# Chunked delta-rule recurrence and block attention of a three-block network: another factoring of the recurrence, attention by pairs of heads

## Reference, cut to what matters

```python
def rwkv7_mixer(ya, ...):            # 6 heads of 64 channels
    ...
    def step(state, inp):
        r_t, w_t, k_t, v_t, kk_t, a_t = inp
        sa = jnp.einsum('bhij,bhj->bhi', state, -kk_t)
        state = (state * w_t[:, :, None, :]
                 + sa[..., :, None] * (kk_t * a_t)[:, :, None, :]
                 + v_t[..., :, None] * k_t[:, :, None, :])
        return state, jnp.einsum('bhij,bhj->bhi', state, r_t)
    ...
def moba_mixer(q, k, v):             # 6 heads of 64 channels
    ...                              # with 2 blocks of 256 keys and top 3, every past block is taken:
                                     # plain causal attention over 512 tokens
```

## Time and profile before

| | us |
|---|---|
| median of 3 runs | 3279.8 (3279.63 to 3281.37) |
| profiled execution, first to last instruction (span) | 3270.9 |
| median less span | 8.9 |
| the stage that changes (first score to last attention output, 1701.8 to 1806.1) | 104.3 |
| PE busy in that stage | 103.22 |
| DVE / ACT busy in that stage | 38.88 / 30.84 |

### The profile page before, as it was taken

How to read it: one execution, slowest core, us unless ns; L and a number is a source line. 1 busy time by engine, 2 the same in 40 slices (tenths; PEclk the granted TensorE clock), 3 DMA queues, 4 the chain that set the end, 5 groups by cost and what they waited for, 6 DMA issues and landing times.

```text
span 3270.9 us, 35828 instructions
## 1 busy us (share of the span) xinstructions
PE 3179.8 (97%) x14634; PEld 1976.4 (60%) x14634; DVE 1372.5 (42%) x2564; ACT 598.2 (18%) x1240; POOL 1.4 (0%) x6
## 2 busy tenths in 40 slices
PE   8999999999999999999999999999999999999998
PEld 5855554334333433458786588888546444688887
DVE  4256530111111111165743364466353894364655
ACT  2143220110010001121442320102332002120001
POOL 0000000000000000000000000000000000000000
PEclk9999999999999999999997999999999999999999
DMA  6122369999999999931000222222111222222221
GB/s 268 60 78 93 114 250 411 428 428 429 429 428 429 429 428 429 428 138 37 26 1 1 93 87 78 86 95 103 55 52 52 77 77 77 77 78 103 78 78 52
DMA packets 43100, 585.39 MB, mean 179 GB/s; under 512 B 4768, under 2 KB 6816, under 8 KB 7648
## 3 DMA queue, kind: packets, MB, share of 16 engines
q1 hardware_dynamic: 42752, 582.45, 43.8%
q0 software_dynamic: 224, 1.18, 0.1%
HBM read 581.51 MB, written 2.10 MB: 178 GB/s over the span
## 4 chain that ended last, share of the span: by engine, by line
PE 87%; DMA 9%; DVE 3%; ACT 1%; issue 1%; SPq 0%; DVEq 0%; ACTq 0%
PE PS L482 20%; PE PS L294 11%; PE PS L1670 11%; PE PS L686 10%; DMA ring<-in_weights 5%; PE PS L1648 4%; DMA A<-in_weights 4%; PE PS L1246 3%; PE PS L374 2%; PE PS L1593 2%; PE PS L348 2%; PE PS L1634 1%; PE PS L1575 1%; PE PS L2198 1%; PE PS L1038 1%; PE PS L1203 1%
## 5 line engine op out<-in xcount | busy, mean ns | idle before, releaser
L482 PE MATMUL PS<-A 128*128 128x256 f32 x1336 | 298.4, 380 | 0.0
L1670 PE MATMUL PS<-ring,A 128*64 128x512 f32 x1248 | 284.8, 599 | 1.5 <-DMA ring<-in_weights 0.6
L482 PEld LDWEIGHTS PS<-A 128*128 128x128 f32 x1336 | 254.1, 190 | 35.1 <-issue 0.8
L294 PE MATMUL PS<-H,ring 128*128 128x512 f32 x544 | 234.4, 593 | 0.7 <-issue 0.7
L1752 DVE TENSOR_TENSOR A<-A,PS 64x512 f32<-64x512 f32 x64 | 44.1, 690 | 434.6 <-ACT A L1699 434.6
L482 PE MATMUL PS<-H,ring 128*128 128x256 f32 x784 | 185.3, 380 | 0.8 <-ACT A L1785 0.8
L1670 PEld LDWEIGHTS PS<-ring,A 128*64 128x64 f32 x1248 | 82.7, 136 | 168.0 <-issue 160.8
L294 PEld LDWEIGHTS PS<-H,ring 128*128 128x128 f32 x544 | 103.5, 190 | 130.0 <-issue 130.0
L1670 PE MATMUL PS<-A 128*64 128x512 f32 x784 | 178.4, 598 | 2.0 <-DMA A<-in_weights 0.8
L686 PE MATMUL PS<-A 128*128 128x256 f32 x800 | 178.7, 379 | 0.0
L1648 PE MATMUL PS<-A 128*64 128x512 f32 x768 | 174.3, 598 | 3.4 <-DMA A<-in_weights 3.1
(11 more groups left out here) (534 smaller groups left out, 4126.9 us busy)
## 6 DMA issues: line engine op xcount, KB each, us to landing
ring<-in_weights SPq DMA_DIRECT2D x176, 2048.0 KB, 14.2
A<-in_weights SPq DMA_DIRECT2D x96, 2048.0 KB, 24.3
X<-in_x SPq DMA_DIRECT2D x1, 2048.0 KB, 12.9
H<-in_weights SPq DMA_DIRECT2D x1, 2048.0 KB, 13.6
A<-in_weights SPq DMA_DIRECT2D x2, 768.0 KB, 23.8
vec<-in_vec SPq DMA_DIRECT2D x1, 1047.0 KB, 11.1
A<-in_ctx SPq DMA_DIRECT2D x1, 1024.0 KB, 19.1
out_y<-X SPq DMA_DIRECT2D x2, 512.0 KB, 2.9
```

The source lines that it names most:

```text
L294: mm = nc.tensor.matmul(bank[:, 0:out_width], weight_tile(name, n), moving(k), start=k == 0, stop=k == k_tiles - 1)
L482: mm = nc.tensor.matmul(pair_bank(name, p, n), w[:, k, :], x[:, k, :], start=k == 0 and not more, stop=k == 3, skip_group_check=more)
L1670: mm = nc.tensor.matmul(PS[CAP * up:CAP * (up + 1), c % 2, :], XS[:, k, CAP * b:CAP * (b + 1)], expert_tile(slot, 8 * (k % 4) + 4 * up), s ...
```

## The change

Recurrence. The walk over the chunks goes. In its place:

- `keys_turned`: 12 transposes bring the decayed keys of `KR` to tokens on partitions; ACT copies them (3 copies of 128x512) to `KTOK`.
- `values_seen`: 24 products (128x128 weights, 64 columns moving), as L2619 before; 4 ACT copies of 128x384 to `WVTOK`.
- `solved`: 24 products of the inverse with 128 columns moving, 64 of `WVTOK` and 64 of `KTOK` side by side; 6 ACT copies of 128x512 into slot 2 of SC2.
- `gains`: 12 products that, with an identity added by DVE, give a 64x64 matrix by head for chunks 1 and 2; the state then goes from chunk to chunk by `carried` (6 products of 64x64 weights with 64 columns, twice), on top of `added` (36 products, as L2633 and L2634 before, three groups of 12). DVE scales each of three states out of PSUM (`state_kept`).
- `queries_solved`: 18 products of 128 rows by 64 columns, 128 moving, which DVE adds to the queries in `KR` (`query_kept`, 3 times).
- `outputs`: by pair of heads, 16 products of 128 rows by 64 columns and then 6 of 64x64 with the states, 128 moving each; 3 ACT copies of 128x512.

Attention. The unit order is now by pair of heads: units 2k and 2k+1 are the same query tile of the two heads of a tile. Step k (12 of them) is: the two scores of step k+1, at k = 4 and 8 the outputs of the last pair (eight matmuls that alternate between the heads), the transposes of unit 2k, a piece of the recurrence, the transposes of unit 2k+1, a second piece. A pair's output leaves in one ACT copy of 128x512. DVE takes normalise and maximum in turn.

```diff
@@ -2288,53 +2288,92 @@
...
+        def moba_place(u):
+            return 2 * (u // 8) + u % 2, u % 8 // 2
+
...
+            if u >= 2:
+                pe.wait_ge(S["att_exp"], u - 1)
...
+        def moba_output(pe, p):
+            pe.wait_ge(S["att_turned"], 8 * p + 8)
+            if p:
+                pe.wait_ge(S["att_heads"], p)
             for kt in range(TT):
...
+                for h in (2 * p, 2 * p + 1):
+                    mm = nc.tensor.matmul(PS[half64(h), 7, kt * P:], MVTOK[:, kt, 64 * h:64 * h + 64],
+                                          MPT[h % 2][:, kt, kt * P:], start=kt == 0, stop=True, skip_group_check=kt > 0)
             mm.then_inc(S["att_out"], 1)
...
+        def moba_step(pe, k, first, second):
+            if k + 1 < UNITS2 // 2:
+                moba_score(pe, 2 * k + 2)
+                moba_score(pe, 2 * k + 3)
+            if k and k % 4 == 0:
+                moba_output(pe, k // 4 - 1)
+            moba_turn(pe, 2 * k)
+            first()
+            moba_turn(pe, 2 * k + 1)
+            second()
...
+        def moba_step_act(act, k):
+            for u in (2 * k, 2 * k + 1):
+                moba_turned_act(act, u)
                 if u + 2 < UNITS2:
...
+                    moba_exp_act(act, u + 2)
+            if k and k % 4 == 0:
+                moba_leave_act(act, k // 4 - 1)
+
...
+        def moba_step_dve(dve, k):
+            for u in (2 * k, 2 * k + 1):
+                moba_normalise_dve(dve, u)
                 if u + 2 < UNITS2:
...
+                    moba_max_dve(dve, u + 2)
@@ -2483,8 +2522,10 @@
...
-        WU = (a(46)[:, 0:384], a(47)[:, 0:384])
-        STATE = a(48)[:, 0:192].rearrange("p (a i) -> p a i", a=3)
+        KTOK, WVTOK = tok384(A[:, 46:49, :]), tok384(A[:, KT2:KT2 + 3, :])
+        GAIN = a(46)[:, 0:384].rearrange("p (c a i) -> p c a i", c=2, a=3)
+        EYE64 = a(47)[:, 0:64]
@@ -2604,47 +2645,107 @@
...
+            def keys_turned(p):
+                for c in range(4):
+                    mm = nc.tensor.transpose(PS[:, p, c * P:(c + 1) * P], KR[p][:, c, 0, :], ident)
+                mm.then_inc(S["formed"], 1)
+
+            def values_seen(c):
...
+                for h in range(6):
+                    i = slice(64 * h, 64 * h + 64)
+                    mm = nc.tensor.matmul(PS[:, c % 3, i], SC2[h][:, c, 2, :], TOK2[0][:, c, i], start=True, stop=True)
+                mm.then_inc(S["formed"], 1)
...
+            def solved(h):
...
+                    tile, at = divmod(384 * c + 64 * h, T)
+                    both = A[:, KT2 + tile:47 + tile:43, at:at + 64]
+                    mm = nc.tensor.matmul(PS[:, (h + 1) % 3, c * P:(c + 1) * P], SC2[h][:, c, 0, :], both,
+                                          start=True, stop=True)
+                mm.then_inc(S["formed"], 1)
...
+            def gains():
...
+                for c in (1, 2):
+                    for h in range(6):
+                        mm = nc.tensor.matmul(PS[half64(h), 1, 192 * c - 192 + 64 * (h // 2):192 * c - 128 + 64 * (h // 2)],
+                                              SC2[h][:, c, 2, 64:], TOK2[1][:, c, 64 * h:64 * h + 64], start=True, stop=True)
+                mm.then_inc(S["chain"], 1)
...
+            def added(bank, at, c, opens):
+                for src in range(2):
+                    for h in range(6):
+                        i = slice(64 * h, 64 * h + 64)
+                        l, r = (TOK2[1][:, c, i], SC2[h][:, c, 2, 0:64]) if src == 0 else (TOK2[2][:, c, i], TOK2[0][:, c, i])
+                        mm = nc.tensor.matmul(PS[half64(h), bank, at + 64 * (h // 2):at + 64 * (h // 2) + 64], l, r,
+                                              start=opens and src == 0 and h < 2, stop=True,
+                                              skip_group_check=not (opens and src == 0 and h < 2))
+                mm.then_inc(S["chain"], 1)
...
+            def carried(c, bank, at):
+                pe.wait_ge(S["state"], c + 1)
+                for h in range(6):
+                    rows, p = half64(h), h // 2
+                    mm = nc.tensor.matmul(PS[rows, bank, at + 64 * p:at + 64 * p + 64], GAIN[rows, c - 1, p, :],
+                                          STATES[c - 1][rows, p, :], start=False, stop=True, skip_group_check=True)
+                mm.then_inc(S["chain"], 1)
...
+            def queries_solved(p):
...
+                for c in (1, 2, 3):
+                    for h in (2 * p, 2 * p + 1):
+                        mm = nc.tensor.matmul(PS[half64(h), 2, (c - 1) * P:c * P], SC2[h][:, c, 2, 64:], SC2[h][:, c, 1, :],
+                                              start=True, stop=True)
+                mm.then_inc(S["query"], 1)
...
+            def outputs(p, part):
+                if part == 0:
...
+                    for src in range(2):
+                        for c in range(4):
+                            for h in (2 * p, 2 * p + 1):
+                                l = TOK2[0][:, c, 64 * h:64 * h + 64] if src == 0 else SC2[h][:, c, 2, 0:64]
+                                nc.tensor.matmul(PS[half64(h), p, c * P:(c + 1) * P], l, SC2[h][:, c, 3 - 2 * src, :],
+                                                 start=src + c == 0, stop=True, skip_group_check=src + c > 0)
...
+                    for c in (1, 2, 3):
+                        for h in (2 * p, 2 * p + 1):
+                            rows = half64(h)
+                            mm = nc.tensor.matmul(PS[rows, p, c * P:(c + 1) * P], STATES[c - 1][rows, p, :],
+                                                  KR[p][rows, c, 1, :], start=False, stop=True, skip_group_check=True)
+                    mm.then_inc(S["y_chunk"], 1)
...
+                keys_turned(p)
+            moba_step(pe, 0, lambda: values_seen(0), lambda: values_seen(1))
+            moba_step(pe, 1, lambda: values_seen(2), lambda: values_seen(3))
+            for k in range(3):
+                moba_step(pe, 2 + k, lambda: solved(2 * k), lambda: solved(2 * k + 1))
+            moba_step(pe, 5, gains, lambda: (added(0, 0, 0, True), added(0, 192, 1, False)))
+            def last_added():
+                pe.wait_ge(S["state"], 1)
+                added(1, 0, 2, True)
+            moba_step(pe, 6, lambda: queries_solved(0), last_added)
+            moba_step(pe, 7, lambda: carried(1, 0, 192), lambda: queries_solved(1))
+            moba_step(pe, 8, lambda: carried(2, 1, 0), lambda: queries_solved(2))
+            for p in range(3):
+                moba_step(pe, 9 + p, lambda: outputs(p, 0), lambda: outputs(p, 1))
@@ -2748,21 +2849,38 @@
...
+            moba_exp_act(act, 0)
+            for p in range(2):
+                keys_kept(p)
+            moba_exp_act(act, 1)
+            keys_kept(2)
+            for k in range(12):
+                moba_step_act(act, k)
+                if k < 2:
+                    values_kept(2 * k)
+                    values_kept(2 * k + 1)
+                elif k < 5:
+                    solved_kept(2 * k - 4)
+                    solved_kept(2 * k - 3)
+                elif k >= 9:
+                    outputs_kept(k - 9)
@@ -2885,25 +3003,40 @@
...
+            def state_kept(c, bank, at):
+                d = PS[:, bank, at:at + 192].rearrange("p (a i) -> p a i", a=3)
+                nc.vector.tensor_tensor(STATES[c], d, SCL[:, :, c:c + 1].to_broadcast([P, 3, 64]), ALU.mult
+                                        ).then_inc(S["state"], 1)
...
+            def query_kept(p):
+                dve.wait_ge(S["query"], p + 1)
+                nc.vector.tensor_tensor(KR[p][:, 1:, 1, :], KR[p][:, 1:, 1, :], as_tiles(PS[:, 2, 0:384]), ALU.add
+                                        ).then_inc(S["query_out"], 1)
...
+            for k in range(12):
+                moba_step_dve(dve, k)
+                if k == 5:
+                    dve.wait_ge(S["chain"], 1)
+                    link(dve, "dve", nc.vector.tensor_tensor(EYE64, ident[:, 0:64], ident[:, 64:], ALU.add))
+                    nc.vector.tensor_tensor(GAIN.rearrange("p c a i -> p (c a) i"),
+                                            PS[:, 1, 0:384].rearrange("p (n i) -> p n i", n=6),
+                                            EYE64.unsqueeze(1).to_broadcast([P, 6, 64]), ALU.add).then_inc(S["state"], 1)
                     dve.wait_ge(S["decays"], 4)
...
+                    dve.wait_ge(S["chain"], 3)
+                    state_kept(0, 0, 0)
+                if k == 6:
+                    query_kept(0)
+                if k == 7:
+                    dve.wait_ge(S["chain"], 5)
+                    state_kept(1, 0, 192)
+                    query_kept(1)
+                if k == 8:
+                    dve.wait_ge(S["chain"], 6)
+                    state_kept(2, 1, 0)
+                    query_kept(2)
+            dve.wait_ge(S["y_kept"], 3)
             for p in range(3):
                 dve.wait_ge(S["pe_sums"], Y_SUMS + p + 1)
```

(50 more changed lines are left out.)

150 lines of the change are left out of this document (46 added, 104 removed).

## The result

| | before | changed |
|---|---|---|
| median, us | 3279.72 (4 runs) | 3236.46 (4 runs, 3235.25 to 3237.76) |
| profiled execution: own time / span | not recorded / 3270.9 | 3237.76 / 3236.0 |
| the stage | 104.3 | 65.3 |

Ratio 0.9868, 95% interval 0.9854 to 0.9882: 43 us or 1.3% less. The forecast was 3248, range 3239 to 3262: right in direction, but the gain came out 43 us and not 32, and the time lies 2.5 us under the range. Eight later executions of the changed kernel (e12, e13) gave 3229.3 to 3237.8.

The account below looks back on a forecast made before the run. PE, busy 97% of the span, was taken as the bound. Stage: work 53.2, waits 6, clock 13, together 72.2 against 104.3 us; profiled execution 3270.9 to 3238.9, plus 8.9 to the median, 3248 us, range 3239 to 3262.

Parts of the forecast that it names:

- PE's work, 53.2: In the stage, PE's products counted as if always at 2.4 GHz: 53.2 us after the change, against 82.6 before.
- The first rival: Attention scores: the two scores of a pair do not overlap, about 7.5 us more, 3255.5; chance 0.15.
- the twelve score pairs together: Attention scores: two heads' scores run side by side on different row halves, 8.8 us in all, 15.2 if serial.
- The change of shapes: Recurrence: alternating products of 64 and 128 weight rows take 0.36 us each at 2.4 GHz; among their like, about 0.11.
- Row halves in one bank in turn: Rival for `carried` and the second part of `outputs`: row halves in one PSUM bank take turns, 2.8 us more, 3250.8; chance 0.09.
- Waits, 6: In the stage, PE waits 6 us: 4 for late DVE and ACT steps, 2 at the start; 1.1 before.
- Clock, 13: Stage start: half clock lasts until the middle of step 4's attention outputs, adding 16 us, hiding 3 of waits: 13.
- the rival of the early rise: Stage: the clock rises already within `solved` at step 2, 7.5 us less, 3240.5; chance 0.12.
- The three other falls go: Stage: the stretches that preceded three of the four clock falls are gone; granted clock 1.0 after step 4.
- 8.9 us between span and median, taken as constant: Whole execution: the profiled span lies 8.9 us under the median, so 3238.9 becomes 3248.
- The hand-overs win: Rival: short PE waits in every step make the clock fall again, steps 5 to 8 and later, 10 us, 3258; chance 0.13.
- the clock never rises: Rival, slower than before: all PE work in the stage takes 1.2 GHz time, stage 115 us, 3290.5; chance 0.03.

Follow-up runs that it names:

- e12: The changed kernel, unchanged, run again: three executions at 3229.3 to 3229.7 us and one at 3236.4.
- e13: The changed kernel, unchanged, run once more in the same rounds as a repeat of e4: four executions at 3235.5 to 3237.8 us, median 3236.59.
- e4: The changed kernel plus eight 128x128 identity products into an idle bank ahead of the first score: 3232.65 us, stage 57.6.
- e6: The kernel of e4 with the second score of each pair waiting for the end of the first: 3235.80 us.
- e7: The kernel of e4 with the recurrence's outputs in the old order, the 64x64 state product between the two of 128 rows: 3243.03 us.
- e3: The kernel before, keeping its old walk over the chunks, with only the new attention by pairs of heads: 3253.05 us, ratio 0.9919.
- e2: The changed kernel with attention put back to single heads, so only the recurrence is new: 3254.25, 3254.35, 3239.54 and 3238.32 us.
- e8: The kernel before plus the eight identity products of e4 ahead of its first score: 3273.36 us, ratio 0.9982.
- e1: The kernel before, run again without edit: 3280.68 us, ratio 1.0004; profiled execution 3281.21 with a span of 3279.4.

## Why the prediction was right or wrong

**Where the time went.** The stage gave 39.0 us in the two profiled executions, and the prediction's own split can now be filled in: work at 2.4 GHz 82.6 to 55.3 (e4), clock 20.6 to 7.7 (65.3 against 57.6), waits 1.1 to 2.3. It said 53.2, 13 and 6.

- *PE's work, 53.2*: right in sum, 4% low. Outputs in pairs took 2.30, `solved` 0.22 each, `outputs` 0.12, a 512-key score pair 1.11, as said. The first rival (pairs do not overlap) is refuted by e6. What was low is the twelve score pairs together: from start to start on PE they take 11.8 us in e4, and the sum has 8.8; transposes take 9.1 and the sum has 10.2, every other term is within 0.4. In three of the pairs (two of 128 keys, one of 256) the second score waits for ACT's exp. A pair of 128 keys so lasts 1.04 us and not the 0.49 of the first one, and the profile counts all of it as busy (in the chain after these are the lines 1744.72 and 1745.55; here are ACT's exp and such a pair in the timeline of e4):

```profile
1716.74 0.69 ACT L2334 ACTIVATE A<-PS,small 128x512 f32<-128x512 f32 x1
1717.01 1.04 PE L2299 MATMUL PS<-ring,A 64*128 64x128 f32 x4
```

- *The change of shapes*: right, and shown by e7: 11.9 us, where 18 x (0.94 - 0.33) = 11 were expected.
- *Row halves in one bank in turn*: refuted. Six products of 64 rows by 64 columns into one bank take 0.80, a start included; in turn six would take 6 x 0.213 = 1.28 (128 columns at twice the 0.107 of a pair). The Trainium skill (TensorEngine Tiling (Array Packing), Restrictions and Gotchas) says that different row tiles cannot access the same bank simultaneously; for tiles that write different partition halves this trace disagrees, by the 0.80 us against 1.28.
- *Waits, 6*: wrong, 2.3 in e4 and 1.1 in the changed kernel. The step that failed was to set each engine's lateness down as PE's idle time. The chain does pass through DVE and ACT, for 5.8 us, but PE stands idle for 1.1 us of the stage: in the rest of that time it has scores, transposes or pieces of the recurrence already released. Part of the lateness is inside the score pairs above.
- *Clock, 13*: wrong in size, the term that was mis-sized most within the stage: 7.7. The step that failed was the choice of what ends the stretch: it ended at the last products of the first `solved` (1726.0, step 2) and not in step 4's outputs. That was the rival of the early rise, and its stage, 64.7, is within 0.6 of 65.3. Of the two candidates for the rise I took the later without a row that spoke against the earlier. And in 3 of 12 executions it ended after 3.4 us. So the first fall remained, as said, but not with one length.
- *The three other falls go*: right. e3 keeps w and has them, e2 and the changed kernel do not; e8 keeps them at the w pieces though the first is removed. All twelve such falls in four profiles (before, e1, e3, e8) came inside a w piece or at most 1.1 us behind it. That it is w's alternation of row counts, and not something else in that walk, is argued from the place alone: no run puts w's pieces by themselves into the new kernel, and the alternation of y, put back by e7, brought no fall.
- *8.9 us between span and median, taken as constant*: wrong. An execution's own time is 1.8 above its span; the profiled one of before was itself 7.1 us better than the median, mostly by isolated falls behind the stage that it did not have (e1). Summed up: stage 6.9 less than forecast, this 7.1, and 4.1 more outside the stage give 3247.8 - 14.0 + 4.1 = 3237.9 for the profiled execution, which took 3237.76. The 7.1 and the 4.1 belong together, since both are mainly falls that come in some executions and not in others, so that the error outside the stage is 3.0 net and the stage's 6.9 is the larger part: clock 5.3, waits 3.7, less the 2.1 by which PE's work was low. That falls elsewhere add or take some us was no term of the sum.
- *The hand-overs win* and *the clock never rises*: neither. No second fall came in the stage in any profile of the new recurrence.

What stays open is why the first stretch lasts 3.4 us in some executions and 20.5 in most of the same kernel. By fine windows it began 0.8 us behind the first score in the one profile (e12, 1704.1) and 1.4 and 1.2 us behind it in the two others (1705.5, and 1705.1 in e13); the order of the work is the same. This distance alone does not settle it: in the kernel before it is 0.9 us, and the stretch lasts 17.1. Open too is why isolated falls behind the stage come in some executions and not in others.

## What to carry to other kernels

Put products of one tile shape in runs of their own and let neighbours go to opposite halves: the same 66 products cost 0.1 or 0.3 us each by their order alone. Size a change in a stage with clock falls by what it does to the falls as well, and name for each fall the work that stood ahead of it. Before a sum is set against a median, find out which execution the profile is: a span's distance from the median is not a constant. Here the constant was 7.1 us off, and only because falls elsewhere cost the execution after 4.1 us was the net error 3.0.

## What the runs showed that was not expected

- One kernel has two times 7 us (e12) or 15 us (e2) apart on the same chip; between profiles of the changed kernel the length of one stretch at 1.2 GHz makes 7.2 us of stage. Four executions can all show one side.
- Four products of no use (0.9 us) in a wait of 1.95 us did as much as eight: with either the stage ran at 2.4 GHz in all ten profiles.
- Four outputs of one head followed by four of the other, 3.86 us with the gap, overlap at the seam, so by-head order costs 1.56 us a pair and not 2.1.
